# Heads 2 and 3 of a retention trunk advance their state every 128 rows instead of every 256

## What is computed

```python
def retention_chunk(q, k, v, s, log_gamma):
    scores = jnp.einsum('bhid,bhjd->bhij', q, k) * decay[None]
    inner = jnp.einsum('bhij,bhjv->bhiv', scores, v)
    cross = jnp.einsum('bhid,bhdv->bhiv', q_dec, s)
    s_new = jnp.exp(log_gamma * C)[None, :, None, None] * s + jnp.einsum('bhjd,bhjv->bhdv', k_dec, v)
    return inner + cross, s_new
```

## Time and profile before

| what | us |
|---|---|
| median of three runs | 2850.07 |
| lowest and highest of them | 2849.48, 2850.29 |
| the profiled execution, its own time | 2851.84 |
| its span (first to last instruction) | 2850.0 |
| PE busy | 2803.0 (98%) |
| DVE busy | 1808.7 (63%) |
| ACT busy | 1127.2 (40%) |

### The profile page before, as it was taken

How to read it: one execution, slowest core, us unless ns; L and a number is a source line. 1 busy time by engine, 2 the same in 40 slices (tenths; PEclk the granted TensorE clock), 3 DMA queues, 4 the chain that set the end, 5 groups by cost and what they waited for, 6 DMA issues and landing times.

```text
span 2850.0 us, 36714 instructions
## 1 busy us (share of the span) xinstructions
PE 2803.0 (98%) x13504; PEld 2252.7 (79%) x13504; DVE 1808.7 (63%) x2588; ACT 1127.2 (40%) x1901; POOL 685.1 (24%) x456
## 2 busy tenths in 40 slices
PE   6999999999999999999999999999999999999998
PEld 5888888888877777777777787877887788778876
DVE  7657566667555365555666656775677667766775
ACT  5444444444564433443444433333333333333332
POOL 4343433435332233434343320000000000000000
PEclk9999999999999999999999999999999999999999
DMA  4544444444564344453544456477547754775496
GB/s 143 192 148 154 172 148 155 158 175 150 177 231 141 112 153 161 163 183 110 194 143 151 158 238 251 163 270 306 210 163 267 305 215 160 270 297 223 154 341 254
DMA packets 281849, 552.80 MB, mean 194 GB/s; under 512 B 24216, under 2 KB 166872, under 8 KB 270527
## 3 DMA queue, kind: packets, MB, share of 16 engines
q1 hardware_dynamic: 266279, 541.73, 53.3%
q10 hardware_dynamic: 15168, 8.46, 1.0%
q0 software_dynamic: 224, 0.26, 0.0%
HBM read 375.59 MB, written 175.14 MB: 193 GB/s over the span
## 4 chain that ended last, share of the span: by engine, by line
PE 92%; DVE 4%; issue 2%; DMA 1%; ACT 1%; POOL 1%; ACTq 0%; SPq 0%; DVEq 0%; POOLq 0%
PE bank L1309 29%; PE bank L1311 28%; PE bank L1310 28%; PE bank L1359 2%; PE bank L1382 1%; PE bank L1501 1%; DVE w_lo L2172 1%; PE bank L1631 1%; DVE xa_lo L2172 0%; PE bank L1619 0%; PE bank L1609 0%; DVE xs L2186 0%; PE bank L1304 0%; DMA x_d<-x_out 0%; DMA raw<-in_w_branch_pool 0%
## 5 line engine op out<-in xcount | busy, mean ns | idle before, releaser
L1309 PE MATMUL bank<-xa_hi,wa_hi 128*128 128x512 f32 x2240 | 889.7, 397 | 4.6 <-ACT part_s L1863 3.1
L1310 PE MATMUL bank<-xa_lo,wa_hi 128*128 128x512 f32 x2240 | 874.2, 390 | 0.0
L1311 PE MATMUL bank<-xa_hi,wa_lo 128*128 128x512 f32 x2240 | 874.2, 390 | 0.0
L1309 PEld LDWEIGHTS bank<-xa_hi,wa_hi 128*128 128x128 f32 x2240 | 421.2, 188 | 107.2 <-issue 22.7
L1311 PEld LDWEIGHTS bank<-xa_hi,wa_lo 128*128 128x128 f32 x2240 | 420.9, 188 | 90.4
L1310 PEld LDWEIGHTS bank<-xa_lo,wa_hi 128*128 128x128 f32 x2240 | 421.5, 188 | 82.9
L2172 DVE TENSOR_TENSOR wa_lo<-w_raw,wa_hi 128x512 fp32r<-128x512 f32 x320 | 312.7, 979 | 166.0 <-ACT wa_hi L1856 165.2
L2172 DVE TENSOR_TENSOR wa_lo<-w_sum,wa_hi 128x512 fp32r<-128x512 f32 x240 | 194.2, 809 | 241.3 <-ACT wa_hi L1856 241.3
L2172 DVE TENSOR_TENSOR w_lo<-raw,w_hi 128x512 fp32r<-128x512 f32 (+1 forms) x288 | 181.9, 658 | 197.1 <-ACT w_hi L1970 197.1
L1856 ACT ACTIVATE wa_hi<-w_raw 128x512 fp32r<-128x512 f32 x320 | 201.1, 628 | 242.5 <-PE bank L1311 238.3
L1970 ACT ACTIVATE w_hi<-raw 128x512 fp32r<-128x512 f32 (+1 forms) x288 | 166.6, 603 | 315.2 <-PE bank L1311 222.7
(11 more groups left out here) (253 smaller groups left out, 4322.9 us busy)
## 6 DMA issues: line engine op xcount, KB each, us to landing
w_raw<-in_w_in SPq DMA_DIRECT2D x80, 1024.0 KB, 5.3
v_d<-turned SPq DMA_DIRECT2D x64, 512.0 KB, 3.2
qk_s<-qk_d SPq DMA_DIRECT2D x32, 1024.0 KB, 7.5
v_s<-v_d SPq DMA_DIRECT2D x32, 1024.0 KB, 11.6
raw<-in_w_branch_ret SPq DMA_DIRECT2D x128, 256.0 KB, 4.7
tabs<-in_c_rope SPq DMA_DIRECT2D x16, 1024.0 KB, 6.8
qk_d<-high SPq DMA_DIRECT2D x32, 512.0 KB, 4.6
qk_d<-c_low SPq DMA_DIRECT2D x32, 512.0 KB, 5.4
```

What stands on the lines that cost most here:

```text
L1309: pe.matmul(out, lh, rh, start=first, stop=False, skip_group_check=onto)
L1310: pe.matmul(out, lh, rl, start=False, stop=False, skip_group_check=onto)
L1311: return pe.matmul(out, ll, rh, start=False, stop=last, skip_group_check=onto)
```

## The change

`chunk(h)` is 256 for heads 0 and 1 and 128 for heads 2 and 3. The decay factors in the tables and in `new_state` follow it. In heads 2 and 3 there are now four updates and four outputs of 128 rows each. An update of 128 rows has 6 matmuls, an output 6 with the state (none in the very first of block 0) and 3 with scores. `scores` itself is as before, so the block of scores between the two halves of 256 rows is still computed, but no longer used.

In these heads `turn_og(hb - 1)` comes first, and it waits for `y_added` bank by bank instead of for all four. `branch(hb - 1, 0)` is cut in two halves around the third update and output. ACT and DVE get the additional splits of the state and the additional `new_state` in their order, and DVE's `og_low` is apart from `gate_og`. `updates` and `splits` count for the semaphores.

```diff
+def chunk(h):
+    return CHUNK if h < 2 else P
+
...
     rope = np.zeros((HEADS, 2, NS, P, 2, 2 * T), np.float32)
     for h in range(HEADS):
+        local = np.arange(SEQ) % chunk(h)
         for i, scale in enumerate((g[h] ** (local + 1.0), g[h] ** -(local + 1.0) * DK ** -0.5)):
...
         def turn_scale(j):
-            return float(gamma[JOBS[j][1]] ** CHUNK) if kind(j) == "k" else 1.0
+            return float(gamma[JOBS[j][1]] ** chunk(JOBS[j][1])) if kind(j) == "k" else 1.0
...
+        def updates(hb, c):
+
+            b, h = divmod(hb, HEADS)
+            return sum(T // chunk(i) for i in range(HEADS)) * b + sum(T // chunk(i) for i in range(h)) + c
...
+            def short_update(hb, i):
+                s, c, j = hb % 2, i // 2, i % 2
+                if j == 0:
+                    pe.wait_ge(tv_arrived[s][c], 32 * (hb // 2 + 1))
+                if i:
+                    pe.wait_ge(st_new, 2 * updates(hb, i))
+                else:
+                    pe.wait_ge(sc_masked, 2 * hb + 2)
+                for d in range(2):
+                    w = slice(d * P, (d + 1) * P)
+                    split_product(banks[6 + d][:, :], kt_s[s][:, c, 0, j, w], kt_s[s][:, c, 1, j, w],
+                                  v_s[s][:, c, 0, j, :], v_s[s][:, c, 1, j, :], True, True).then_inc(up_mm, 1)
+
+            def short_output(hb, i):
+                s, c, j = hb % 2, i // 2, i % 2
+                cross = i or hb >= HEADS
+                if cross:
+                    pe.wait_ge(st_lo_done, splits(hb, i) + 1)
+                pe.wait_ge(sc_lo_done, 2 * hb + c + 1)
+                pe.wait_ge(normed, 4 * hb + max(i - 1, 0))
+                out = banks[j][:, :]
+                q = slice(i * P, (i + 1) * P)
+                if cross:
+                    for d in range(2):
+                        split_product(out, qk_s[s][:, 0, 0, d, q], qk_s[s][:, 0, 1, d, q],
+                                      st_hi[:, d, :], st_lo[:, d, :], d == 0, False)
+                k = slice(j * CHUNK + j * P, j * CHUNK + (j + 1) * P)
+                split_product(out, sc_hi[:, c, k], sc_lo[:, c, k], v_s[s][:, c, 0, j, :], v_s[s][:, c, 1, j, :],
+                              not cross, True).then_inc(o_mm, 1)
+
             def turn_og(hb):
-                if hb:
-                    pe.wait_ge(y_added, KT * hb)
                 if hb % HEADS == 0:
                     pe.wait_ge(sc_masked, 2 * hb + 4)
                 pe.wait_ge(normed, 4 * hb + 4)
                 for vt in range(4):
+                    if hb:
+                        pe.wait_ge(y_added, KT * hb - 3 + vt)
                     for i in range(NT):
                         mm = pe.transpose(banks[2 + vt][:, i * P:(i + 1) * P], og[:, i, vt * P:(vt + 1) * P], ident[:])
                     mm.then_inc(ogt_mm, 1)
...
-                    update(hb, 0)
-                    output(hb, 0)
-                    if h:
+                    if chunk(h) == P:
                         turn_og(hb - 1)
-                    update(hb, 1)
-                    if h:
-                        branch(hb - 1, 0)
+                        short_update(hb, 0)
+                        short_output(hb, 0)
+                        short_update(hb, 1)
+                        short_output(hb, 1)
+                        branch(hb - 1, 0, range(2))
+                        short_update(hb, 2)
+                        short_output(hb, 2)
+                        branch(hb - 1, 0, range(2, 4))
+                        short_update(hb, 3)
+                        short_output(hb, 3)
                     else:
...
+                    act.wait_ge(st_new, 2 * updates(hb, c))
+                    if c > 1 or hb >= HEADS:
+                        act.wait_ge(o_mm, 4 * hb + c * chunk(hb % HEADS) // P)
...
+                    if chunk(h) == P:
+                        og_high(hb - 1, range(3))
+                        state_high(hb, 1)
+                        og_high(hb - 1, range(3, 4))
+                        state_high(hb, 2)
...
-                        highs(b, (h - 1) * UH, 4)
+                        highs(b, (h - 1) * UH, 2)
+                        if chunk(h) == P:
+                            state_high(hb, 3)
+                        highs(b, (h - 1) * UH + 2, 2)
...
+                    if chunk(h) == P:
+                        gate_og(hb - 1, range(3))
+                        new_state(hb, 0)
+                        gate_og(hb - 1, range(3, 4))
+                        state_low(hb, 1)
+                        og_low(hb - 1)
+                        new_state(hb, 1)
+                        statistics(hb, 0)
+                        state_low(hb, 2)
+                        output_bias(hb, 0)
+                        new_state(hb, 2)
+                        lows(b, (h - 1) * UH, 2)
+                        state_low(hb, 3)
+                        lows(b, (h - 1) * UH + 2, 2)
+                        add_y(hb - 1, 0, range(2))
+                        new_state(hb, 3)
+                        add_y(hb - 1, 0, range(2, 4))
```

More of the change, by code:

```diff
@@ L1502, in turn_og, with branch @@
                     mm.then_inc(ogt_mm, 1)
-            def branch(hb, p):
+            def branch(hb, p, vts=range(4)):
                 b, h = hb // HEADS, hb % HEADS
@@ L1509, in branch @@
                     pe.wait_ge(y_added, KT * hb + 4)
-                for vt in range(4):
+                for vt in vts:
                     if p == 0:
@@ L1737, in _ @@
                     hb = b * HEADS + h
-                    update(hb, 0)
-                    output(hb, 0)
-                    if h:
+                    if chunk(h) == P:
                         turn_og(hb - 1)
-                    update(hb, 1)
-                    if h:
-                        branch(hb - 1, 0)
-                    else:
-                        scores(hb + 1)
-                    output(hb, 1)
+                        short_update(hb, 0)
[8 more added lines that the diff above has]
+                        short_output(hb, 3)
+                    else:
+                        update(hb, 0)
+                        output(hb, 0)
+                        if h:
+                            turn_og(hb - 1)
+                        update(hb, 1)
+                        if h:
+                            branch(hb - 1, 0)
+                        else:
+                            scores(hb + 1)
+                        output(hb, 1)
                     if 0 < h < HEADS - 1:
@@ L2001, in normalize, with og_high @@
                                    bias=norm_bias[:, i:i + 1]).then_inc(normed, 1)
-            def og_high(hb):
-                for vt in range(4):
+            def og_high(hb, vts):
+                for vt in vts:
                     act.wait_ge(og_gated, 4 * hb + vt + 1)
@@ L2098, in _ @@
                     hb = b * HEADS + h
-                    state_high(hb, 1)
-                    if h:
-                        og_high(hb - 1)
+                    if chunk(h) == P:
[3 more added lines that the diff above has]
+                        state_high(hb, 2)
+                    else:
+                        state_high(hb, 1)
+                        if h:
+                            og_high(hb - 1, range(4))
                     normalize(hb, 0)
@@ L2460, in gate_og, with add_y @@
                     tt(z_lo[s][:, vt, :], z_in[s][:, vt, :], og_hi[:, vt, :].bitcast(F32), ALU.subtract, og_lo_done)
-            def add_y(hb, p):
-                for c in range(4):
+            def add_y(hb, p, some=range(4)):
+                for c in some:
                     d = 4 * p + c
@@ L2731, in _ @@
[L2731 to L2736, removed]
+                    if chunk(h) == P:
[15 more added lines that the diff above has]
+                        add_y(hb - 1, 0, range(2, 4))
+                    else:
+                        new_state(hb, 0)
+                        statistics(hb, 0)
+                        if h:
+                            gate_og(hb - 1)
+                            og_low(hb - 1)
+                        if b and h == 0:
+                            out_variance(b - 1)
+                        output_bias(hb, 0)
+                        if hb == 1:
+                            dve.wait_ge(b_consts_in, 32)
+                        state_low(hb, 1)
+                        new_state(hb, 1)
+                        if b and h == 0:
+                            final(b - 1)
+                        if hb == 1:
+                            for u in range(RAW, LEAD):
+                                low(u)
+                        if h:
+                            lows(b, (h - 1) * UH, 4)
+                            add_y(hb - 1, 0)
```

48 lines of the change are left out of this document (16 added, 32 removed).

## The result

| what | before | with the change |
|---|---|---|
| median of 13 runs each, us | 2850.19 | 2856.47 |
| lowest and highest | 2847.82, 2851.95 | 2854.61, 2857.75 |
| ratio of the times, 95% interval | | 1.0022 [1.0015, 1.0029] |

The change makes the kernel slower by 6.3 us. The forecast was 2857.8 in a range of 2852.5 to 2862.5.

A forecast was written before the change was run, and what follows sets the result against it. PE, busy 98% of the span, was taken as the bound. Blocks 1 to 3 +4.0, block 0 +3.4 and head 3's branch +0.4 gave +7.8 us on 2850.07: 2857.8 us, range 2852.5 to 2862.5.

The forecast's parts named there:

- 36 matmuls less, per head of blocks 1 to 3: Outputs of heads 2 and 3, blocks 1 to 3: fewer matmuls at 0.232 us each, saving 1.39 us per head.
- start: transposes wait for y: Head start, blocks 1 to 3: the fourth transpose bank waits 0.62 us for DVE's adds, 0.72 us with restart.
- second output waits for the split: Output 1, blocks 1 to 3: only update 1 covers the state split; wait 1.24 us, 1.34 us with restart.
- block 0, per head: Block 0, heads 2 and 3: nothing saved; update 1 waits for the state, output 1 for the split; +1.69 us.
- head 3, second half of the branch: Before head 3's branch: DVE's last adds to y slightly late, wait 0.03 us plus restart, 0.1 us in each of four.
- rival "not late": First transposes of six heads: adds to y start early enough, so no wait; 2853.5 us, not slower, chance 0.11.
- rival 2848.0: Output 1: the split of the state hides behind update 1; 2848.0 us, within 0.2%, chance 0.04.
- plain saving of 2841.7: Heads 2 and 3: no wait at all, only the 8.4 us saving; 2841.7 us, faster, chance 0.07.
- third and fourth split hide: Later in the head: half a branch (5.6 us) before each of the last two outputs covers its state split; no wait.
- rival of 2861.8: End of head 3: DVE's adds come 1 us later before the branch, +4 us over four heads; 2861.8 us, chance 0.10.
- rival 2871.4: Heads 2 and 3: PE's granted clock falls after repeated waits, 1.7 us in each of eight heads; 2871.4 us, chance 0.03.
- PE runs through without a gap: Heads 2 and 3 before the change: PE taken as fully dense, busy 42.39 of 42.40 us in head 2 of block 1.

The follow-up runs named there:

- f7: The changed kernel with five unread matmuls between update 1 and output 1 in heads 2 and 3 of blocks 1 to 3; 2856.59 us, ratio 1.0022.
- f2: The changed kernel with a second pair of split-state buffers for odd chunks of heads 2 and 3; 2849.21 us, ratio 0.9996.
- g8: The changed kernel with update 0 ahead of the transposes, 12 branch matmuls between update 1 and output 1, and block 0 long; 2842.90 us, ratio 0.9974.
- f1: The changed kernel with 12 branch matmuls between update 1 and output 1, their operand split ahead of the state; 2847.61 us, ratio 0.9988.

## Why the prediction was right

The time was in the range, and the sign and the places were right; the rise of 6.3 us was 1.5 less than the 7.8 forecast. Its steps, against block 1 and block 0 of the changed kernel:

| step of the prediction | predicted, us | measured, us |
|---|---|---|
| 36 matmuls less, per head of blocks 1 to 3 | -1.39 | -1.39 (6 x 0.232, 36 fewer in the page) |
| start: transposes wait for y | 0.72 | 0.63 |
| second output waits for the split | 1.34 | 1.36 |
| seam before the branch, gone | not seen | -0.24 |
| per head, blocks 1 to 3 | +0.67 | +0.36 by these rows, +0.37 by head 2 of block 1 |
| block 0, per head | +1.69 | 0.71 + 0.98 - 0.24 = +1.45 |
| head 3, second half of the branch | +0.1 | +0.16 |

- **The adds to y are late, bank by bank.** They start 2033.32 - 2032.66 = 0.66 before the branch ends, as in the earlier trace rows. The wait is 0.63, without the restart of 0.10 that I had added: after the transposes the update shows the same 0.31 to its second matmul as behind any run of transposes. The rival "not late" (2853.5) is out.
- **The split doesn't hide.** ACT, DVE and PE came one after the other in 2.37 us (2039.43 to 2041.80), as in the earlier trace rows. f7 fills the hole at no cost, f2 takes its cause away. The rival 2848.0 is out, and with it the plain saving of 2841.7, although g8 comes near it with the same 36 matmuls less.
- **The third and fourth split hide** behind the branch halves, as the prediction said. DVE's last adds before head 3's branch cost 0.16 and not 1, so the rival of 2861.8 is out. Block 3's 0.26 stands in the second output, and its cause stays open.
- **The clock did not fall.** The granted clock is 0.9 or more in every slice, 0.997 on average as in the kernel before, and 1.00 over heads 2 and 3 of each block, with two waits in each head. By the Trainium skill, page "TensorE: Matmul & The Clock Gate", section "A second HAM failure mode: psum-queue depth-cycling", short idle times between groups of matmuls, repeated often, made the gate swing in one kernel. The trace does not agree for this pattern, and f2 and f7, which change the holes, moved by the holes alone. The rival 2871.4 is out.
- **What was wrong.** The step that failed is the reading "PE runs through without a gap". Busy time counts matmuls in flight, and each lasts 0.16 us beyond its slot, so 42.39 of 42.40 hides every seam below that. The unseen 0.24 in eight heads is 1.9 us, and the restart added to the transposes 6 x 0.09 = 0.5; without both the sum is 5.4. Block 3's 0.26 and the 0.06 more in each head 3 (0.24) bring it to 5.9 of the 6.0 in the table of blocks. The 0.26 was not foreseen by any step, so a little of the nearness is luck. Of the named signs, head 3 of block 1 takes 40.16 us (2076.08 to 2116.24) instead of 40.3 to 40.4, and in block 0 it gains 1.6 instead of 1.8; the wait for y is not one of 0.6 in the last bank but is spread over the run of transposes. "PE's busy time shrinks by about the 8.4 us" was wrong too: it fell by 4.8, and my reading, which no run tested, is that tails of flights fill part of each new hole.

## What to carry to other kernels

Before a long step is cut into short ones, write down the whole hand-over chain from the engine that frees the buffer to the one that waits (here 2.6 us over ACT and DVE) and count the work that will stand between; saved matmuls are only worth their time if the chain is covered. Where work from an independent stream can be put between, the same cut turns from 0.22% slower to 0.12% faster (f1), and with the update ahead of the transposes and block 0 left long to 0.26% faster (g8). Cut only where something is saved: block 0 had nothing to gain and cost half of the loss. And read seams as distances from start to start, since busy shares of overlapping instructions don't show them.

## What the runs showed of the hardware

- A run of 16 transposes that waits in the middle for one bank after another loses the wait alone (2.29 us in two kernels, and 1.86 + 0.415 = 2.28 if only the last bank counts), with no restart for each bank, while a single wait before 128x512 matmuls adds 0.08 to 0.11 (0.31 to 0.34 instead of 0.23 to the second matmul; 0.31 behind the seam of 0.16 in the kernel before, 0.34 behind the hole of 1.25).
- PE went on 0.05 us after DVE's copied state was complete (DVE 1752.40 + 1.28 = 1753.68, PE 1753.73), where the row from before had 0.15.
